# A transformer block's fused kernel: another order of ScalarE's and VectorE's work between the latent keys' projection and the latent queries

## The reference, cut to what is computed around the change

There are 256 tokens of 1024 numbers (`x`), 256 tokens of context (`ctx`) and 256 of memory (`mem`), all in fp32. The first block projects both `x` and `ctx` with `w_in` and splits the result; then come attention over latent keys, a two-way retention, an output projection and a convolutional feed-forward. A second block with attention, a recurrence, cross attention on `mem` and another feed-forward follows.

## Time and profile before

| | us |
|---|---|
| median of 3 runs | 856.71 |
| the profiled execution's own time | 853.94 |
| its span, first to last instruction | 852.1 |
| TensorE busy | 824.0 (97%) |
| VectorE busy | 569.5 (67%) |
| ScalarE busy | 448.5 (53%) |
| mean granted TensorE clock | 0.995 of full |

### The profile page before, as it was taken

The page is one execution under the profiler, slowest core; times in us unless marked ns, Lnnn a source line. Parts: engine busy times, 40 slices in busy tenths (PEclk is TensorE's granted clock), DMA queues, the critical chain, the costliest instruction groups (busy, mean ns, idle before and its releaser), DMA issues. The chain is left out here.

```text
span 852.1 us, 12903 instructions
## 1 busy us (share of the span) xinstructions
PE 824.0 (97%) x4992; PEld 714.5 (84%) x4992; DVE 569.5 (67%) x900; ACT 448.5 (53%) x739; POOL 17.1 (2%) x25
## 2 busy tenths in 40 slices
PE   7989797999999999999999999999999999999997
PEld 5779687877899999997889978888977788888885
DVE  1467875797787788788757777577546655655454
ACT  3476317256456566654546584646535644454442
POOL 1001000000000000000000000010000000000000
PEclk9999899999999999999999999999999999999999
DMA  9976451155656666568668654244505565656551
GB/s 334 347 260 224 130 200 46 57 156 166 199 180 212 181 176 184 182 222 286 228 195 286 181 156 135 75 148 157 190 12 162 174 197 174 190 180 196 175 171 50
DMA packets 103668, 152.87 MB, mean 179 GB/s; under 512 B 6538, under 2 KB 55862, under 8 KB 103608
## 3 DMA queue, kind: packets, MB, share of 16 engines
q1 hardware_dynamic: 102112, 149.16, 54.7%
q10 hardware_dynamic: 1496, 2.89, 1.0%
HBM read 150.97 MB, written 1.05 MB: 178 GB/s over the span
## 5 line engine op out<-in xcount | busy, mean ns | idle before, releaser
L2104 DVE TENSOR_TENSOR w_lo<-raw,w_hi 128x1024 fp32r<-128x1024 f32 (+1 forms) x228 | 275.3, 1212 | 148.5 <-ACT w_hi L1539 147.7
L1539 ACT ACTIVATE w_hi<-raw 128x1024 fp32r<-128x1024 f32 (+1 forms) x228 | 238.2, 1050 | 206.1 <-PE bank L754 145.4
L752 PE MATMUL bank<-w_hi,hT_hi 128*128 128x512 f32 (+2 forms) x400 | 158.0, 395 | 6.4 <-DVE w_lo L2104 5.4
L754 PE MATMUL bank<-w_hi,hT_lo 128*128 128x512 f32 (+2 forms) x400 | 153.9, 385 | 0.0
L753 PE MATMUL bank<-w_lo,hT_hi 128*128 128x512 f32 (+2 forms) x400 | 153.7, 384 | 0.0
L855 PE MATMUL bank<-hT_hi,w_hi 128*128 128x256 f32 x512 | 145.2, 284 | 0.0
L857 PE MATMUL bank<-hT_hi,w_lo 128*128 128x256 f32 x512 | 145.2, 284 | 0.0
L856 PE MATMUL bank<-hT_lo,w_hi 128*128 128x256 f32 x512 | 145.2, 284 | 0.0
L857 PEld LDWEIGHTS bank<-hT_hi,w_lo 128*128 128x128 f32 x512 | 97.3, 190 | 0.0
L856 PEld LDWEIGHTS bank<-hT_lo,w_hi 128*128 128x128 f32 x512 | 97.3, 190 | 0.0
L855 PEld LDWEIGHTS bank<-hT_hi,w_hi 128*128 128x128 f32 x512 | 97.3, 190 | 0.0
(11 more groups left out here) (343 smaller groups left out, 1165.7 us busy)
## 6 DMA issues: line engine op xcount, KB each, us to landing
raw<-w_up_dram SPq DMA_DIRECT2D x132, 256.0 KB, 3.4
raw<-w_ada_dram SPq DMA_DIRECT2D x48, 512.0 KB, 4.8
raw<-w_down_dram SPq DMA_DIRECT2D x44, 512.0 KB, 4.4
raw<-w_in_dram SPq DMA_DIRECT2D x40, 512.0 KB, 4.7
raw<-w_gate_dram SPq DMA_DIRECT2D x44, 256.0 KB, 2.9
raw<-w_out_dram SPq DMA_DIRECT2D x16, 512.0 KB, 3.3
raw<-wk_x_dram SPq DMA_DIRECT2D x8, 512.0 KB, 4.7
raw<-wv_x_dram SPq DMA_DIRECT2D x8, 512.0 KB, 3.4
```

The costliest lines, as they stand in the source:

```text
L752: pe.matmul(o, xh, yh, start=first, stop=False, skip_group_check=skip)
L754: return pe.matmul(o, xl, yh, start=False, stop=last, skip_group_check=skip)
L1539: act.activation(unit_view(w_hi[n % NSPLIT], u), unit_view(raw[u % NRAW], u), ACT.Copy).then_inc(w_hi_ready, 1)
L2104: dve.tensor_tensor(unit_view(w_lo[n % NSPLIT], u), unit_view(raw[u % NRAW], u), unit_view(w_hi[n % NSPLIT], u).bitcast(F32), ALU.subtract ...
```

```diff
@@ -135,8 +135,8 @@
 SUMMED = (4, 5, 6, 7, 8, 9, 10, 11)
 GATES = (4, 5, 10, 11)
 SUM_AFTER = {8: (4, 5), 10: (6, 7)}
-SUMS_BESIDE = {**{(name, n): 1 for name in ("rk", "rv") for n in range(4) if name == "rv" or n},
-               ("uq0", 0): 1, ("ukv1", 0): 14,
+SUMS_BESIDE = {**{(name, n): 1 for name in ("rk", "rv") for n in range(4) if name == "rv" or n % 2},
+               ("rv", 3): 2, ("uq0", 0): 1, ("ukv1", 0): 14,
                ("wout1", 0): 1, ("wout1", 1): 1,
                **{(f"down{p}", n): 1 for p, n in ((0, 0), (0, 2), (0, 4), (0, 6), (0, 8), (0, 10), (1, 4), (1, 6))}}
 
@@ -1004,9 +1004,12 @@
             run(rg)
             turn("ctx", None, None, (6, 7, 0, 1))
             run(rq)
+            ckvpe = rows_steps("ckvpe", hT_hi, hT_lo, turn_before("ctx"), cT, b=4)
+            for _ in range(2):
+                next(ckvpe)
             for g in range(2, len(VEC_GROUPS)):
                 turn_vectors(g, g - 2)
-            rows_panel("ckvpe", hT_hi, hT_lo, turn_before("ctx"), cT, b=4)
+            run(ckvpe)
             rk = rows_steps("rk", hT_hi, hT_lo, None, cT, b=0)
             for _ in range(3):
                 next(rk)
@@ -1627,6 +1630,13 @@
             act.wait_ge(csilu_ready, 3)
             free(act.activation(csilu[:, 1, :], csilu[:, 0, :], ACT.Copy), use)
 
+            def xi_tables(d):
+
+                c = (C_XF, C_XB)[d] - C_RCOS
+                for h in range(RH):
+                    act.activation(xi[d][:, h, :], k1[:, c:c + TOK], ACT.Exp,
+                                   scale=lgam[:, 4 * d + h:4 * d + h + 1]).then_inc(xi_ready, 1)
+
             for name, _ in VEC_GROUPS[1]:
                 g, r, n = VEC[name]
                 act.dma_start(vrow[g][r:r + n, :], vec_src[name]).then_inc(in_vec, 16)
@@ -1698,6 +1708,7 @@
             for t in range(T):
                 square("mem", 0, t, row[:, t, :])
 
+            feed_units(last_unit["rk"] + 1)
             act.wait_ge(lb_in_ready, 2)
             act.activation(lbc[:, 1:3, :], lbc[:, 1:3, :], ACT.Exp).then_inc(lb_exp_ready, 1)
             act.wait_ge(in_decay, 16)
@@ -1711,32 +1722,28 @@
                     act.activation(wctx[:, d, h, :], k1[:, C_WEXP - C_RCOS + 2 * d:C_WEXP - C_RCOS + 2 * d + 2],
                                    ACT.Exp, scale=lgam[:, 4 * d + h:4 * d + h + 1]).then_inc(wctx_ready, 1)
             scale_row("mem", row[:, 1, :], row[:, 1, :])
-            feed_one()
             turn("mem")
-            feed("rk")
-            feed("rv")
+            feed("rk", 1)
+            for h in range(RH):
+                act.wait_ge(decay_ready, h + 1)
+                act.activation(decay[:, h, :, :], decay[:, h, :, :], ACT.Exp).then_inc(decay_exp_ready, 1)
+            xi_tables(1)
+            feed("rv", 1)
             turn("cq")
             for t in range(2 * T):
                 use = ("rv", t)
                 ready(act, use)
                 dst = rv_row if t < T else rvc_row
                 free(act.activation(dst[:, t % T, :], ps(use)[:, :], ACT.Copy), use)
-            for h in range(RH):
-                act.wait_ge(decay_ready, h + 1)
-                act.activation(decay[:, h, :, :], decay[:, h, :, :], ACT.Exp).then_inc(decay_exp_ready, 1)
 
             turn("ckv")
             turn("ckvc")
-            for h in range(RH):
-                for d in range(2):
-                    c = (C_XF, C_XB)[d] - C_RCOS
-                    act.activation(xi[d][:, h, :], k1[:, c:c + TOK], ACT.Exp,
-                                   scale=lgam[:, 4 * d + h:4 * d + h + 1]).then_inc(xi_ready, 1)
             for t in range(T):
                 use = ("rT", "rq", t)
                 ready(act, use)
                 free(act.activation(rqT[:, :, t * P:(t + 1) * P],
                                     ps(use)[:, :].rearrange("p (h t) -> p h t", h=RH), ACT.Copy), use)
+            xi_tables(0)
             for p in range(2):
                 feed_units(min(reach(last_unit[f"uq{p}"] + 1), last_unit["ukv1"] + 1))
                 for t in range(T):
@@ -2329,9 +2336,9 @@
                 emptied(dve, ("ckvpe", t))
                 step(rope_mla(kpe_row[:, t:t + 1, :], t, 1))
                 settle()
-            feed_units(fed[0] + 1)
+            feed_units(last_unit["rk"] + 1)
             turn("mem")
-            feed("rk")
+            feed("rk", 1)
             for t in range(T):
                 rope_ret(("rk", t), t, rk_row)
             feed_units(fed[0] + 1)
@@ -2345,13 +2352,14 @@
                                                 wctx[:, d, h, t:t + 1], RET_SCALE, ALU.mult, ALU.mult)
                 free(ins, use)
                 feed_units(fed[0] + 1)
-            feed("rv")
-            for name in ("cq", "ckv", "ckvc"):
-                turn(name)
+            feed("rv", 1)
+            turn("cq")
             for t in range(T):
                 use = ("rT", "rk", t)
                 ready(dve, use)
                 free(dve.tensor_copy(rkT[:, :, t * P:(t + 1) * P], ps(use)[:, :].rearrange("p (h t) -> p h t", h=RH)), use)
+            for name in ("ckv", "ckvc"):
+                turn(name)
             for d in range(2):
                 use = ("rstate", d)
                 ready(dve, use)
```

## The result

The changed kernel takes 845.5 us (median of 4 runs, 845.32 to 846.11), the kernel before 857.37 in the same comparison (4 runs, 855.63 to 858.46): ratio 0.9865, 95% interval 0.9846 to 0.9884. Faster, by 1.35%; forecast were 847.2 us and a range of 843.0 to 852.0. The profiled execution took 845.55 us, its span is 843.7, 8.4 less than before.

The account below looks back on a forecast made before the run. TensorE, busy 97%, was taken as the bound, losing 12.8 us to four waits and a slow clock. With 3.25 left, 9.5 won: 856.71 - 9.5 = 847.2 us, range 843.0 to 852.0.

Parts of the forecast that it names:

- `ckvpe` starts late by: First ckvpe unit, now ahead of the convolution vectors: starts 0.85 us behind the end of rq, waiting for its w_lo.
- its second unit: Second ckvpe unit ahead of the vectors: 0.25 us of new waiting for its w_lo.
- fourth `rk` unit: TensorE's wait for the w_lo of rk's last unit: 0.55 us instead of 4.28.
- `rv`, first and third unit: TensorE's waits for VectorE in rv: 0.2 us at the first unit, a new 0.8 at the third.
- `uq0`: TensorE's wait for cqT_lo before uq0: 0.6 us instead of 3.35, with uq0 starting at 122.8.
- `rstate`: The 1.10 us wait for rkT before rstate: gone, as VectorE copies rkT before the latent keys.
- slow clock in the profile: The slow stretch behind the fourth rk unit's wait, 2.3 us: taken as gone with that wait.
- all left: Sum of the waits expected to remain from ckvpe to uq0: 3.25 us of 12.8.
- Clock once more at half: Rival: a slow stretch comes anyway behind a small wait or the transposes, 2.3 us more, 849.5; chance 0.12.
- VectorE becomes the bound: Rival: uq1 lands late or VectorE's queue has an unseen pause; cqT_lo's wait stays 3.35 us, total 850.0; chance 0.15.
- It doesn't do what it says: Rival: the fourth rk unit's w_lo still stands behind decay and ropes, as late as before; 853.2 us, chance 0.04.
- Slower: Rival: four short waits between 93 and 123 us each bring the clock down; 870 us, chance 0.03.

Follow-up runs that it names:

- filled: The kernel before with 14, 25 and 26 identity transposes by TensorE in three of its four waits; median 853.2 us, ratio 0.9970 to the kernel before.
- undo_vec: The changed kernel with the convolution vectors' transposes back ahead of all of ckvpe; median 847.4 us, stretch 83.44.
- busy: The kernel before with 30 identity transposes between turn mem and the fourth rk unit, in the last bank VectorE frees; median 859.3 us, ratio 1.0052.
- undo_cq: The changed kernel with ukv0 back ahead of turn cq on ScalarE and VectorE; median 849.4 us, stretch 85.76.
- busy2: The kernel before with 25 identity transposes ahead of the fourth rk unit, in the bank of the memory's first pair; median 856.2 us, ratio 0.9989.
- undo_rk: The changed kernel with the fourth rk unit's w_hi back behind the exponentials, its w_lo behind a sum and turn mem; median 848.8 us, stretch 84.83.
- better: The changed kernel with the same work reordered further: ckvpe and rk writes moved, sums put into VectorE's pauses; median 840.9 us, 0.9822 of the kernel before.
- undo_rkt: The changed kernel with VectorE's rkT copies back behind turns ckv and ckvc; median 846.3 us, stretch 82.52.

## Why the prediction was right, step by step

| step | forecast | measured |
|---|---|---|
| `ckvpe` starts late by | 0.85 | 1.05 |
| its second unit | 0.25 | 0.17 (starts 66.14, due 65.97) |
| fourth `rk` unit | 0.55 (93.4 less 92.8 is 0.6) | 0.53 |
| `rv`, first and third unit | 0.2, 0.8 | 0.24, 0.67 |
| `uq0` | 0.6 | 0.35 |
| `rstate` | 0 | 0 |
| slow clock in the profile | 0 | 0 |
| all left | 3.25 | 3.0 |
| won in the profile | 9.5 | 9.93 (stretch), the rest unchanged |

**Which wait ends last.** For each of the four waits the releaser was found, its place in its engine's hand-written order moved, and the next thing that is late worked out. All came out within 0.3 us. VectorE's chain of 30.6 us, summed from rows of the kernel before, ran 93.55 to 124.1, which is 30.6. With the 1.57 us by which this execution's stretch began later taken off, the moments fit too: the `w_lo` of `rk`'s last unit begins at 92.0 (forecast 92.2), `uq0` at 122.7 (122.8).

**The part that was mis-sized** is how the profile stands to the median. I carried the 2.77 us between the profiled execution and the median of the kernel before over to the changed one: 844.4 + 2.77 = 847.2. The changed kernel's profiled execution is its median (845.55 and 845.5): 1.15 above the 844.4, and the median 1.7 below the 847.2. The distance is not a fixed cost of a run: the profiled execution of the kernel before was a short one, shorter than any of 35 further runs of it in the later comparisons (854.1 to 860.0, median 856.2). Part of that is its start: its stretch begins at 55.48, nearly the earliest of the twelve profiles, and 1.57 before the changed kernel's, which is why 9.93 won in the stretch are 8.4 between the spans. Its mean clock of 0.995 is the middle of the 35, and the 15 runs with that clock take 854.1 to 856.8, so the clock doesn't explain its own distance. The clock does tell in the rest of the spread: the 12 runs at 0.990 to 0.993 take 855.6 to 860.0, median 857.3, the 23 above it 854.1 to 856.8, median 855.6, and the four of the changed kernel have 0.998 to 1.000. That the forecast came within 1.7 us of the median rests in part on luck: the carried 2.77 held a short execution and a median of three runs.

By `filled`, the clock is worth 2.4 us at the median, and from its 853.2 to 845.5 are 7.7 us of waits: 12.8 less 2.3 of clock less 3.0 left is 7.5. The 856.2 less 845.5 is 10.7. The first comparison had 11.9 with four runs of the kernel before; I put the difference down to their small number, which isn't shown.

**The rivals.** *Clock once more at half* did not come true: it stands between 0.998 and 1.000 in the changed kernel. But I gave it the wrong ground, "three other waits left the clock alone": `undo_vec`, `busy`, `undo_cq` and `busy2` show that waits of 1.79 and 3.34 us at the same places bring it down as well, in other executions. The rival's chance was too low for that reason; what the change did right was to leave no wait over 1.05 us in the stretch. *VectorE becomes the bound* holds for the order and not for the price: it is the bound from 93 to 124 us, and the load of `uq1` lands 3.4 us after its issue at 115.78, the short end of the earlier trace rows. *It doesn't do what it says* is refuted by the row at 93.55. *Slower* would have needed short waits that bring the clock down. The rule of the Trainium skill named there (TensorE: Matmul & The Clock Gate, "A second HAM failure mode: psum-queue depth-cycling") would have made the changed kernel swing between the levels. It didn't: behind its waits of 0.24 to 1.05 us the profile has the clock at 1.00 throughout the stretch, and the means of its four runs are 0.998 to 1.000. What did bring the clock down in this case were single waits of 1.79 us and more, once in each such profile and not in a swing.

**Open.** Why the clock falls behind one of two waits of like length and not behind the other isn't shown here. At the vectors it fell behind 1.79 us in `undo_vec` and `busy` and stayed up behind 1.76 in the kernel before and `busy2`; before `uq0` it fell behind 3.34 in `undo_cq` and `busy2` and stayed up behind 3.35 in the kernel before and 3.34 in `busy`. The kernel before has mean clocks of 0.990 to 0.997 in its runs, so it varies from one execution to the next of the same program.

## What to carry to other kernels

Where one engine is busy 97% of the time, read its few waits with their releasers, and for each ask what stands ahead of the releaser in its own engine's order and doesn't need to; then sum the releaser's queue to see what is late next. A wait that is set by the release of a buffer (`ukv0`'s) should have nothing behind it that somebody needs sooner. Put filler work, such as sums, where the helping engine has a pause: three sums moved into pauses were among the moves that brought another 4.6 us (3.5 in the stretch).

## What the runs showed of the hardware

TensorE's clock fell to the lower of its two levels behind idle times of 1.79, 3.34 and 4.28 us, for some 3 to 5 us of work, at 1.5 to 2.4 us each (1.5 in `undo_vec`, 1.6 in `undo_cq`, 1.75 in `undo_rk`, 2.36 before), and stayed up behind others of 1.76, 3.14, 3.34 and 3.35 us. In the kernel before it fell while TensorE still stood still (0.83 from 91.6 to 97.8). The kernel with several such waits has runs 3.6 to 5.8 us apart, the same kernel with transposes in its waits 1.3, and `better` 1.2. The clock isn't all of the spread: `undo_rkt`, with means of 0.998 and 0.999, has runs 3.1 us apart, and `undo_vec`, with the fall, 0.3. Putting back a wait of 1.79 us cost 2.3 us of the stretch, where the order alone accounts for 0.76. And 14, 25 and 26 transposes of the identity in three waits kept the clock up: they were worth 0.3% of a kernel whose arithmetic they don't touch.
